# Two heads share one out-projection at the end of a hybrid decoder block's mixer

## The reference, cut to what matters

```
q, k, v, gate_b, gate_c, u = split(h @ w_in)            # h: normed, modulated x
q, k = apply_rope(q), apply_rope(k)                      # 4 heads, 2 maps each, 64 wide
o = (softmax(q1 k1^T) - lam * softmax(q2 k2^T)) @ v      # causal, blocks of 128 queries
o = rmsnorm(o, subln_g) * (1 - lambda_init)              # per head, 128 wide
y = rmsnorm(gate_b * conv3(gate_c * u))                  # 8 channel groups
x = x + gate2 * (concat([o, y]) @ w_out)
```

## Time and profile before

| | |
|---|---|
| median of 3 runs | 1973.76 us |
| profiled execution, own time | 1973.44 us |
| its span, first to last instruction | 1971.4 us |
| mean granted TensorE clock | 0.973 |
| TensorE busy | 1849.3 us (94%) |
| VectorE busy | 1283.9 us (65%) |
| ScalarE busy | 781.5 us (40%) |
| GpSimd busy | 260.3 us (13%) |

### The profile page before, as it was taken

One profiled execution on the slowest core, in us unless ns is written; L12 is line 12 of the kernel. 1 busy time (PEld: TensorE's weight loads), 2 busy tenths in 40 slices (PEclk: granted clock), 3 DMA queues, 4 the chain that ended last, 5 costly groups with the idle time before them and its releaser, 6 DMA issues.

```text
span 1971.4 us, 22949 instructions
## 1 busy us (share of the span) xinstructions
PE 1849.3 (94%) x8248; PEld 1475.7 (75%) x8248; DVE 1283.9 (65%) x1978; ACT 781.5 (40%) x1401; POOL 260.3 (13%) x400
## 2 busy tenths in 40 slices
PE   3699999999999999999998998789999999999997
PEld 0478888888788877788876675567888888878885
DVE  2677777777576776444325767787766666657677
ACT  2543333333344455111125545474333333334445
POOL 1012112121111000000303330001211111121000
PEclk8799999999999999999999999989999999999998
DMA  7136556565575421111211100223555454387432
GB/s 305 43 115 206 203 203 223 183 214 210 192 260 159 118 80 65 54 33 54 65 46 41 43 21 1 97 86 134 196 178 172 173 180 175 128 278 213 139 97 91
DMA packets 100496, 269.76 MB, mean 137 GB/s; under 512 B 13088, under 2 KB 13472, under 8 KB 100256
## 3 DMA queue, kind: packets, MB, share of 16 engines
q1 hardware_dynamic: 60976, 144.20, 21.6%
q0 software_dynamic: 33728, 115.37, 17.6%
q10 hardware_dynamic: 5680, 8.73, 1.5%
HBM read 209.53 MB, written 54.53 MB: 134 GB/s over the span
## 4 chain that ended last, share of the span: by engine, by line
PE 82%; DVE 9%; ACT 3%; DMA 2%; issue 2%; ACTq 1%; POOL 1%; DVEq 0%; POOLq 0%
PE PS L1425 58%; PE PS L1421 23%; DMA X<-x_t 1%; DVE X L1230 1%; DVE NMax L1331 1%; PE PS L1829 1%; ACTq L798 1%; DMA TmpA<-TmpA 1%; DVE SqSum L1199 1%; DVE Wl L930 0%; POOL TmpA L518 0%; ACTq L727 0%; DVE TmpA L1217 0%; DVE AdaSum L1176 0%; POOL NextQ L521 0%
## 5 line engine op out<-in xcount | busy, mean ns | idle before, releaser
L1425 PE MATMUL PS<-Bh,Wh 128*128 128x512 f32 x1120 | 442.6, 395 | 5.5 <-ACT T L596 5.5
L1425 PE MATMUL PS<-Bl,Wh 128*128 128x512 f32 x1120 | 441.9, 395 | 0.0
L1425 PE MATMUL PS<-Bh,Wl 128*128 128x512 f32 x1120 | 441.2, 394 | 0.0
L1425 PEld LDWEIGHTS PS<-Bh,Wh 128*128 128x128 f32 x1120 | 210.5, 188 | 57.5 <-DVE Wl L930 6.3
L1425 PEld LDWEIGHTS PS<-Bh,Wl 128*128 128x128 f32 x1120 | 210.6, 188 | 50.3
L1425 PEld LDWEIGHTS PS<-Bl,Wh 128*128 128x128 f32 x1120 | 210.5, 188 | 49.2
L1425 PE MATMUL PS<-Wh 128*128 128x512 f32 x616 | 240.3, 390 | 3.4 <-DVE Wl L965 1.7
L1425 PE MATMUL PS<-Wl,Wh 128*128 128x512 f32 x616 | 239.7, 389 | 0.0
L1425 PE MATMUL PS<-Wh,Wl 128*128 128x512 f32 x616 | 239.7, 389 | 0.0
L962 DVE TENSOR_TENSOR Wl<-RawB,Wh 128x512 fp32r<-128x512 f32 x154 | 106.6, 692 | 136.5 <-ACT Wh L571 135.3
L571 ACT ACTIVATE Wh<-RawB 128x512 fp32r<-128x512 f32 x154 | 97.3, 632 | 229.9 <-PE PS L1425 229.9
(11 more groups left out here) (169 smaller groups left out, 2915.9 us busy)
## 6 DMA issues: line engine op xcount, KB each, us to landing
Raw<-up_w SPq DMA_DIRECT2D x88, 512.0 KB, 5.6
Ada<-ada POOLq DMA_DIRECT2D x72, 512.0 KB, 4.4
g_dram<-T SPq DMA_DIRECT2D x88, 256.0 KB, 2.4
W2s<-down_w POOLq DMA_DIRECT2D x88, 256.0 KB, 4.4
s_dram<-W2s POOLq DMA_DIRECT2D x88, 256.0 KB, 2.6
GQ<-g_dram POOLq DMA_DIRECT2D x88, 256.0 KB, 3.4
RawB<-s_dram SPq DMA_DIRECT2D x88, 256.0 KB, 2.9
RawB<-down_w SPq DMA_DIRECT2D x66, 256.0 KB, 2.8
```

The source lines that it names most:

```text
L1425: return nc.tensor.matmul(out, lhs, rhs, start=first, stop=last, skip_group_check=True)
```

## The change

Head 2's out-projection is not spread over the last head's steps any more. At the mixer's end heads 2 and 3 are projected together: a tile is six matmuls into one bank and one addition. Head 3's output is split into slot 1 of Gh and Gl, head 2's stays in slot 0. `out_job` gets a helper `out_part` that does the matmuls of chosen slots without signalling. Behind the last values product PE does slot 0's three matmuls of tiles 0 to 3 into banks 0 to 3, which held scores before, then the turn of head 3; then tiles 0 to 3 get slot 1's three matmuls, and tiles 4 to 15 all six. The counters per head fall by 4 jobs and 4 additions, 16 in all.

```diff
-TILES_LAST = (0, 0, 2, 2, 2, 3, 2, 0, 5)
...
-            def o_hi(h, bank, count):
+            def o_hi(h, bank, count, f=0):
...
-                o_hi(h, 4 + h, (HEADS - 1) * NH)
+                o_hi(h, 4 + h, (HEADS - 1) * NH, 1)
...
-                    for _ in range((TILES if nxt else TILES_LAST)[i] if prev else 0):
-                        add_out(J + (4 if nxt else 0), 1, tile, 6 + tile % 2)
+                    for _ in range(TILES[i] if prev and nxt else 0):
+                        add_out(J + 4, 1, tile, 6 + tile % 2)
...
-            left = TILES_LAST[-1]
-            for t in range(NH * KT - left, NH * KT):
-                if t == NH * KT - 2:
-                    norm_o(HEADS)
-                add_out(JOBS["end"] - 2 * 16, 1, t, 6 + t % 2)
+            norm_o(HEADS)
...
-            def out_job(bank, ns, t):
+            def out_part(bank, ns, t, fs):
...
-                for f, n in enumerate(ns):
+                for f in fs:
+                    n = ns[f]
...
-                made.then_inc(job_done, 1)
+                return made
+
+            def out_job(bank, ns, t, fs=None):
+                out_part(bank, ns, t, range(len(ns)) if fs is None else fs).then_inc(job_done, 1)
...
             values(QB - 1, HEADS - 1)
-            for t in range(NH * KT - TILES_LAST[-1], NH * KT):
-                pe.wait_ge(evac, EVAC["end"] - 2 * 16 + t - 1)
-                out_job(6 + t % 2, (U_WO2,), t)
+
+            pe.wait_ge(exp_done, HEADS * QB * 2)
+            pe.wait_ge(g_ready, GDONE["end"] - NH)
+            pe.wait_ge(lo_done, U_WO2 + 2)
+            for t in range(4):
+                out_part(t, (U_WO2, U_WO2 + 1), t, (0,))
             turn_o(4, HEADS)
-            pe.wait_ge(lo_done, U_WO2 + 2)
...
-                out_job(t % BANKS, (U_WO2 + 1,), t)
+                out_job(t % BANKS, (U_WO2, U_WO2 + 1), t, (1,) if t < 4 else (0, 1))
```

More of the change, by code:

```diff
@@ L48 @@
 for _now, _next, _n, _j, _e, _a, _g in (("conv", "v", 2, 28, 24, 4, 4), ("v", "att", 1, 12, 4, 4, 0),
-                                        ("att", "end", HEADS, 19, 16, 0, 2)):
+                                        ("att", "end", HEADS, 15, 12, 0, 2)):
     JOBS[_next] = JOBS[_now] + _n * _j
@@ L57 @@
 TILES = (0, 0, 0, 0, 0, 5, 6, 5)
-TILES_LAST = (0, 0, 2, 2, 2, 3, 2, 0, 5)
 FIRST = 3
-assert sum(CHUNKS) == 2 * NH * KT and sum(TILES) == sum(TILES_LAST) == NH * KT
+assert sum(CHUNKS) == 2 * NH * KT and sum(TILES) == NH * KT
 STEP_OF_JOB, STEP_OF_JOB_FIRST = [
@@ L838, in root_o @@
                     .then_inc(oroot_done, 1)
-            def o_hi(h, bank, count):
+            def o_hi(h, bank, count, f=0):
                 act.wait_ge(ot_done, count + h + 1)
-                nc.scalar.activation(Gh[:, 0, half(h)], PS[:, bank, :], ACT.Copy, scale=SubG[:, 0:1]).then_inc(ghi, 1)
+                nc.scalar.activation(Gh[:, f, half(h)], PS[:, bank, :], ACT.Copy, scale=SubG[:, 0:1]).then_inc(ghi, 1)
             def body(hh, nq, ny, prev, nxt):
@@ L1353, in norm_o, with o_lo @@
                     .then_inc(onorm_done, 1)
-            def o_lo(h, bank, count):
+            def o_lo(h, bank, count, f=0):
                 dve.wait_ge(ghi, count + h + 1)
-                nc.vector.scalar_tensor_tensor(Gl[:, 0, half(h)], PS[:, bank, :], SubG[:, 0:1],
-                                               Gh[:, 0, half(h)].bitcast(F32), ALU.mult, ALU.subtract).then_inc(g_ready, 1)
+                nc.vector.scalar_tensor_tensor(Gl[:, f, half(h)], PS[:, bank, :], SubG[:, 0:1],
+                                               Gh[:, f, half(h)].bitcast(F32), ALU.mult, ALU.subtract).then_inc(g_ready, 1)
             def body(hh, nq, ny, prev, nxt):
@@ L1392, in _ @@
             body(HEADS - 1, None, U_WO2, True, False)
-            left = TILES_LAST[-1]
-            for t in range(NH * KT - left, NH * KT):
-                if t == NH * KT - 2:
-                    norm_o(HEADS)
-                add_out(JOBS["end"] - 2 * 16, 1, t, 6 + t % 2)
+            norm_o(HEADS)
             for h in range(NH):
-                o_lo(h, 4 + h, GDONE["att"] + (HEADS - 1) * NH)
+                o_lo(h, 4 + h, GDONE["att"] + (HEADS - 1) * NH, 1)
             for t in range(NH * KT):
@@ L1783, in tiles @@
                             pe.wait_ge(lo_done, ny + 1)
-                            if nxt:
-                                pe.wait_ge(rraw, hh * 4 + 8)
+                            pe.wait_ge(rraw, hh * 4 + 8)
                         if t % KT == 0:
-                            pe.wait_ge(g_ready, G + (t // KT + 1 if nxt else NH))
+                            pe.wait_ge(g_ready, G + t // KT + 1)
                         if t >= 2:
@@ L1814, in body @@
                     chunks(n)
-                    n = (TILES if nxt else TILES_LAST)[i] if prev else 0
+                    n = TILES[i] if prev and nxt else 0
                     split = [min(2, n), int(n > 2), int(n > 3), max(n - 4, 0)]
```

## The result

The changed kernel takes 1976.61 us (median of 20 runs, 1973.35 to 1981.44), the kernel before 1973.32 (20 runs, 1971.28 to 1976.16). The ratio is 1.0015, 95% interval 1.0008 to 1.0022: slower by 3.3 us, less than the 0.2% that the prediction called the same, but clear of zero. The forecast was 1974.3, with a range from 1968.8 to 1979.2 that holds the measured time. Its direction held (+0.75 in the sum), its size did not: two terms for the clock and the one for the last stage's pace were too small.

A forecast was written before the change was run, and what follows sets the result against it. The prediction took TensorE to bound the kernel as a whole and VectorE the last out-projection. Its terms, -3.45 + 1.25 + 2.1 + 0.85 = +0.75 us, led to 1974.3 us, range 1968.8 to 1979.2.

The forecast's parts named there:

- The waits: Last head's steps 2 to 7 and the norm behind: waits due to the moved tiles and additions vanish, saving 3.45 us.
- The early matmuls and their waits: Behind the last values product: 12 early matmuls hidden by O's normalisation, their three waits all met; cost 0.
- The last stage's pace: Last out-projection: PE with 84 matmuls sets the pace instead of VectorE, stage 22.5 us; +1.25 us.
- rival D: Last stage stays VectorE's, costing nothing there; 1968.7 to 1970 us; chance 0.14.
- The clock in the steps: Steps 4 to 6: longer PE idle times lower the clock for transposes and scores; 60% of 3.5 us, +2.1.
- theory 2: From the experiments: the clock's stretches are incidental, and the exchange between the engines paces the steps; no chance given.
- upper bound: Clock cost in the steps: 5.7 us, when the scores of steps 3 and 4 are hit as well.
- lower end: Clock in the steps: -1.3 us if the kernel's present low stretch at 1252 went away.
- The clock at the last stage's start: PE idles around turn_o, and a low clock then costs up to 1.7 us; half a chance, +0.85.
- A: Waits' gain is taken back by the end's PE pace and the clock; 1971.5 to 1976.5 us; chance 0.42.
- B: The clock keeps its level through the steps: -2.2 us, 1971.3; chance 0.22.
- C: PE does all steps and the end's start at the lower clock, costing 8.3: +6.1 us, 1979.6; chance 0.22.

The follow-up runs named there:

- e10_full_fill: After with unread matmuls in all of PE's idle times of the last head and around the last turn; 1968.96 us, ratio 0.9973.
- e6_before_fill: Before with 17 unread matmuls: 5 and 4 in step 1, 4 in step 6, 4 behind the last turn; 1968.32 us, ratio 0.9981.
- experiment 3: After with slot 0's product left out of tiles 4 to 15 of the last stage (36 matmuls less); 1973.71 us, ratio 1.0001.
- e1_fill_steps: After with 29 unread matmuls in PE's idle times of steps 1, 4, 5 and 6 of the last head; 1971.22 us, ratio 0.9990.
- experiment 4: Before with head 2's 16 additions and the waits for them left out, its 48 matmuls kept in place; 1972.02 us, ratio 0.9991.
- experiment 9: After, unaltered, measured and profiled again; 1975.78 us, ratio 1.0010 to before.
- experiments 8: After with slot 0's matmuls of six tiles early, not four, plus 42 unread matmuls in PE's idle times; 1967.89 us, ratio 0.9979.
- experiment 2: After with 4 unread matmuls ahead of the last head's turn and 4 behind it; 1975.49 us, ratio 1.0009.
- e7_six_early: After with slot 0's matmuls of six tiles ahead of the last stage, not four, and no unread matmuls; 1972.97 us, ratio 1.0002.

## Why the prediction was right, and where its sizes were off

**The waits, forecast 3.45 us.** Right in sum against before's own profile once the clock is full, but partly by luck. Before against e10_full_fill: 1.51 in block 3 to 4 (forecast 1.35), 0.27 in 4 to 5 (0.4), 0 in 5 to 6 (0), 0.92 in 6 to 7 (0.9), and at the norm 0.80 (0.8; from e6_before_fill's 15.31 to 14.51): 3.5 us. But 1.14 of the first is no wait for a tile: e6_before_fill keeps all tiles and has 4.66 there. The six tile matmuls of step 2 ran at half clock in before, and the fills in step 1 cured it. The prediction took their length from the rows and did not see the low clock in it. At an equal full clock the steps and the norm gain 2.4 us.

**The early matmuls and their waits, forecast 0.** Right. They followed the values product without an idle time in every profile of after's kind, and turn_o started when O was ready.

**The last stage's pace, forecast +1.25.** Right in kind (experiment 3), under-sized: 22.97 (experiment 10) against 21.28 (experiment 6) is +1.7. The 84 matmuls and the mean took the 20.3 us forecast (21.9 less the 1.6 of the low stretch). The rest is behind them: the last addition started 0.4 us behind the last matmul's end (1290.46), because VectorE does the spread of the first half (L1205, L1207) just ahead of the last two. From the last addition to the last square sum it then took 2.14 us (1290.82 to 1292.96), where the sum had 2.06. In the timeline of VectorE in after:

```profile
1288.41 0.68 DVE L1198 TENSOR_TENSOR SqSum<-SqSum,Sq 128x512 f32<-128x512 f32 x1
1289.01 0.17 DVE L1205 RECIPROCAL Inv<-Root 128x4 f32<-128x4 f32 x1
1289.22 0.43 DVE L1207 COPY Spread<-Inv 128x512 f32<-128x512 f32 x1
1289.56 0.74 DVE L1229 SCALAR_TENSOR_TENSOR X<-PS,Gate,X 128x512 f32<-128x512 f32 x1
1290.22 0.68 DVE L1198 TENSOR_TENSOR SqSum<-SqSum,Sq 128x512 f32<-128x512 f32 x1
1290.82 0.74 DVE L1229 SCALAR_TENSOR_TENSOR X<-PS,Gate,X 128x512 f32<-128x512 f32 x1
```

The Trainium skill, "TensorE: Matmul & The Clock Gate", section "Wait — 56ns, not 53.3ns?", has 215.7 ns from start to start, the figure of rival D. The measurement differs and decides: the matmuls started 0.230 us apart in after too (1272.16 to 1283.64 in 50 of them), and the stage was never below 22.9 us with 84 of them.

**The clock in the steps, forecast +2.1.** This is the term that was mis-sized most. After against e10_full_fill, the five distances lose 3.6 us (30.7 against 27.1); that the fills take it away (experiments 1 and 10) rules theory 2 out. The sum lacked two things. First, the clock is low from 1214 on and stays low through the scores of steps 2 and 3 (2.63 and 2.66 us for 1.69 and 2.27 in e1_fill_steps): 1.3 us in the two distances. The prediction had step 3 in its upper bound alone, and step 2 nowhere. That this comes from the missing tiles is not shown: experiment 4 has all tiles and the same low stretch, and before, too, has low stretches there, with a break between them. Second, I took 60% of a cover that came out near full in one step: the score matmuls of block 7 were at half clock from end to end. Its lower end, the low stretch at 1252 going away, didn't come: 15.93 us up to the last stage are 1.4 above the 14.51 of e10_full_fill, before's 16.81 are 1.5 above e6_before_fill's.

**The clock at the last stage's start, forecast 0.85 as half of 1.7.** In the first profile it came, and the stage lost 1.6 (24.55 against 22.95); in the second it didn't. As a mean the term stands on two profiles.

**The terms together, by the table.** Before to after at full clock (67.85 to 64.57) is -3.5 for what was forecast as waits (1.1 of it clock), -1.5 of before's own low stretch and +1.7 of the last stage: -3.3. From there to after's first profile (71.19) it is +3.6 in the steps, +1.4 up to the last stage and +1.6 at its start: +6.6. The sum is +3.3, where the prediction had +0.75; 1.5 of the gap are in the steps' clock, 0.75 at the stage's start, 0.45 in its pace.

**The rivals.** A, the forecast, ended at 1976.5, and 1976.61 is just above it: the mechanism was A's, the clock's price was larger. B (the clock keeps its level, 1971.3) is what the fills make of the kernel; with -2.2 forecast for it, -3.3 found against before's profile and -0.7 at an equal full clock (64.57 against 65.27), it owed its size to before's own lost clock. C's mechanism, low clock in most steps and at the start of the end, came in part, at some 5 us in the first profile (3.6 and 1.6), not the 8.3 of its full price. Block 2's exp ends anywhere from 1216.0 to 1221.9 in the twelve profiles, through code that differs by the fills of step 1 alone (worth up to 0.7 us there). Part of that is the low stretch near 795: seven of the profiles have the full clock there, before and experiment 9 the short stretch, after and experiments 4 and 10 the longer one, and each of the two steps costs 1.6 us. What decides which comes, and the 0.5 us behind the restart, stay open.

## What to carry to other kernels

Here work that filled TensorE's idle times, in a loop where the engines wait for each other, held its clock up, so moving that work away had a price that no sum of waits showed: look at PEclk in the stretches on both sides of the move, and at what the engine will do in the gap. Before judging a change in such a loop, bring both kernels to full clock with matmuls that nobody reads: here that made the change worth 0.7 us, and the clock 2.6 us of before's profile and 6.6 of after's first (67.85 and 71.19 against 65.27 and 64.57). The 0.7 is the difference of two profiles; the ratios, 0.9973 and 0.9981, agree with it and cannot show it. And when two engines have 1.28 and 0.69 us per tile, doubling the second makes it the bound: give some of its work to an earlier idle time (6 tiles early and not 4 took 1.4 us off the last stage in the profiles; the times of experiments 8 and 10 do not show it).

## What the runs showed of the hardware

Matmuls without a use, in PE's idle times, cost nothing that can be seen, and most of them shortened the kernel: 29 of them in the steps took after from ratio 1.0015 to 0.9990, 17 took before to 0.9981. Five of them ahead of the transposes in step 1 brought those from 1.97 us to 1.38 in e1_fill_steps. I had expected them to help before by 1.5 us at most. Around the last turn (experiment 2) their gain is within the noise.

The low stretches move from execution to execution of one kernel, in the changed part and ahead of it, and the time moves: after's 20 runs spread over 8.1 us, before's 20 over 4.9, e10_full_fill's 8 over 4.9. The Trainium skill, "TensorE: Matmul & The Clock Gate", section "HAM oscillation — how this bites in real kernels", tells of a loop whose matmul bursts each start cold after a wait; here it is the same in small, with idle times of 1.9 to 3.1 us, and the price was 0.5 to 2.1 us for each step that met it (after and e7_six_early against e10_full_fill). Not every such wait was met by it: see the 2.64 us of experiment 9.
